# Expert weights in a mixture-of-experts stage: the order in which the queue is given the transfers

## The reference

```python
def expert_block(args):
    e, tok, g = args
    xb = ht[tok]
    hid = jax.nn.silu(xb @ w1[e]) * (xb @ w3[e])
    return (hid @ w2[e]) * g[:, None].astype(ht.dtype)
```

## Time and profile before

| | |
|---|---|
| median of 3 runs | 1514.43 us |
| profiled execution, its own time | 1511.4 us |
| its span, first to last instruction | 1509.6 us |
| TensorE busy | 1363.3 us (90%) |
| VectorE, ScalarE busy | 749.1 us (50%), 483.1 us (32%) |
| matmuls of L1577, of L1591 | 414.6 us, 201.0 us |
| weight DMAs (L742) | 192 of 1 MB, median 14.5 us from issue to landing |
| on the chain that ended last | L1577 8%, weight DMAs 5%, L1591 3% |

### The profile page before, as it was taken

How to read it: one execution, slowest core, us unless ns; L and a number is a source line. 1 busy time by engine, 2 the same in 40 slices (tenths; PEclk the granted TensorE clock), 3 DMA queues, 4 the chain that set the end, 5 groups by cost and what they waited for, 6 DMA issues and landing times. The chain is left out here.

```text
span 1509.6 us, 22993 instructions
## 1 busy us (share of the span) xinstructions
PE 1363.3 (90%) x6898; PEld 626.2 (41%) x6899; DVE 749.1 (50%) x1430; ACT 483.1 (32%) x771; POOL 126.7 (8%) x176
## 2 busy tenths in 40 slices
PE   4999998999988999999999499899899798998991
PEld 2555553445442333333333244488644232332330
DVE  2699999977773221222111453367647242233324
ACT  4101010134323442334232330266522153253421
POOL 0000000001220010011010300000002010010002
PEclk9999999899998999999999699999999899999996
DMA  9645581738059999698834500130094799999925
GB/s 348 203 161 176 187 306 42 287 119 292 29 203 362 384 398 397 242 331 327 298 125 153 204 1 0 41 73 2 2 364 144 287 347 395 397 382 395 398 103 181
DMA packets 163844, 342.73 MB, mean 227 GB/s; under 512 B 9120, under 2 KB 34320, under 8 KB 163792
## 3 DMA queue, kind: packets, MB, share of 16 engines
q1 hardware_dynamic: 146464, 298.03, 54.5%
q0 software_dynamic: 7440, 25.43, 4.6%
q10 hardware_dynamic: 9888, 18.62, 3.6%
HBM read 311.80 MB, written 30.24 MB: 227 GB/s over the span
## 5 line engine op out<-in xcount | busy, mean ns | idle before, releaser
L1577 PE MATMUL PS<-WR,XT 128*64 128x512 f32 x1760 | 414.6, 615 | 26.4 <-DVE WR L1713 16.9
L1577 PEld LDWEIGHTS PS<-WR,XT 128*64 128x64 f32 x1760 | 127.7, 141 | 263.1 <-issue 208.8
L1646 ACT ACTIVATE WR<-WR 128x2048 f32 x90 | 168.9, 1906 | 152.3 <-issue 142.8
L1725 DVE TENSOR_TENSOR HID<-PS,SIL 128x256 f32<-128x256 f32 x55 | 23.3, 424 | 364.1 <-ACT SIL L1657 364.1
L1591 PE MATMUL PS<-WR,HTT 128*64 128x512 f32 x880 | 201.0, 599 | 2.5 <-DVE HTT L1787 1.3
L1245 PE MATMUL PS<-HT,RING 128*128 128x512 f32 (+1 forms) x480 | 159.2, 494 | 0.7 <-DVEq L1368 0.5
L1713 DVE COPY WR<-WR 128x2048 f32 x90 | 108.2, 1228 | 98.4 <-DMA WR<-in_moe_w 40.3
L1392 DVE SCALAR_TENSOR_TENSOR AR<-AR,cols 128x783 f32 (+3 forms) x131 | 122.6, 936 | 0.0
L1245 PEld LDWEIGHTS PS<-HT,RING 128*128 128x128 f32 x480 | 91.0, 190 | 67.0 <-issue 61.1
L1392 DVE SCALAR_TENSOR_TENSOR ROWS<-AR,cols,ROWS 128x783 f32<-128x783 f32 (+2 forms) x123 | 115.1, 936 | 0.0
L1941 PE MATMUL PS<-RING,HT 128*128 128x512 f32 x224 | 99.5, 601 | 3.1 <-DVE HT L524 1.8
(11 more groups left out here) (249 smaller groups left out, 1388.8 us busy)
## 6 DMA issues: line engine op xcount, KB each, us to landing
WR<-in_moe_w SPq DMA_DIRECT2D x192, 1024.0 KB, 14.5
RING<-in_w_mod SPq DMA_DIRECT2D x24, 2048.0 KB, 15.0
moe_out<-YO ACTq DMA_DIRECT2D x110, 128.0 KB
RING<-in_conv_pw SPq DMA_DIRECT2D x16, 512.0 KB, 5.3
moe_out<-HT SPq DMA_DIRECT2D x16, 512.0 KB, 8.5
RING<-in_attn_w_qkv SPq DMA_DIRECT2D x3, 2048.0 KB, 12.8
ROWS<-rows_of_layer SPq DMA_DIRECT2D x11, 512.0 KB, 5.9
RING<-in_conv_pw SPq DMA_DIRECT2D x2, 2048.0 KB, 10.4
```

The source lines that it names most:

```text
L1577: ins = pe.matmul(PUV[g * SUB:(g + 1) * SUB, :], XT[:, k, :], W13[:, :, k, g * (FE // 2):(g + 1) * (FE // 2)], start=(k == 0), stop=(k == ...
L1646: return nc.scalar.activation(to, src, ACT.Copy)
L1725: nc.vector.tensor_tensor(HID[:, :], PUV[:, FE // 2:FE], SIL[:, :], ALU.mult).then_inc(hid_ready[L], 1)
```

## The change

The loop on SP runs over e from 2 to 16. It gives out the pair of expert e and then the down weights of expert e-1. The wait of each load is still for the copy that frees its home: `(e - 1) * 2` for the pair, and e-2 for the down weights of expert e-1. The number of transfers, their sizes and their homes are the same, and so are the instructions of every other engine. The loop's last round gives out only w2 of expert 15.

```diff
-                for e in range(1, NE):
-                    for kind, placed in ((1, (w1_placed,)), (3, (w3_placed,)),
-                                         (2, (w2_placed_low, w2_placed_high))):
-                        if kind != 2 and e <= L + 1:
-                            continue
-                        if e >= 3:
-                            for one in placed:
-                                sp.wait_ge(one[L], (e - 1) * (1 if kind == 2 else 2))
-                        load_weight(sp, L, e, kind)
+                for e in range(2, NE + 1):
+                    if L + 1 < e < NE:
+                        for kind, placed in ((1, w1_placed), (3, w3_placed)):
+                            if e >= 3:
+                                sp.wait_ge(placed[L], (e - 1) * 2)
+                            load_weight(sp, L, e, kind)
+                    if e >= 4:
+                        sp.wait_ge(w2_placed_low[L], e - 2)
+                        sp.wait_ge(w2_placed_high[L], e - 2)
+                    load_weight(sp, L, e - 1, 2)
```

## The result

The changed kernel took 1519.84 us, the median of 7 runs (1518.58 to 1521.36), against 1514.43 for 7 runs of the kernel before on the same chip (1509.93 to 1516.75): ratio 1.0046, 95% interval 1.0033 to 1.0058. The ratio is estimated from the single runs and is not the quotient of the two medians, which is 1.0036; in microseconds the medians differ by 5.4, and the interval stands for 5.0 to 8.8. The change is slower, and just outside my range. Its profiled execution took 1520.53 (span 1518.8). The file is one line longer: up is L1578 now (L1577 before), down L1592 (L1591), the hidden values' take L1663, the weight copies L1647 (ScalarE) and L1714 (VectorE).

The account below looks back on a forecast made before the run. Full DMA stretches in both layers bound the kernel, where queue place sets TensorE's waits. Layer 0 -1.2 us plus layer 1 0.0 made -1.2 on a median of 1514.4: 1513.2 us forecast, range 1507.5 to 1519.5.

Parts of the forecast that it names:

- the advance: How much earlier SP's whole weight queue runs in the new order: 5.4 us in layer 1, 6.7 us in layer 0.
- The advance, layer 1: Layer 1's queue runs 5.4 us earlier: 4.5 at w2 of expert 2 plus 0.9 at the pair behind the gap.
- The advance, layer 0: Layer 0's queue runs 6.7 us earlier: w2 of expert 2 ends at 492.0, old place filled at 497.8, plus 0.9.
- wait of 1.3 at expert 6: Layer 0, down of expert 6: w2 ready at 562.7, TensorE there at 561.4, so it waits 1.3 us.
- VectorE's chain: VectorE waits for w2's upper half with its product of hidden values behind it; the half comes about in time, no cost.
- The sum: Layer 0 -1.2 us plus layer 1 0.0 us gives -1.2 us on the profiled execution of 1511.4.
- The third: Rival: no queue advance, HBM bounds the total, place alone decides; +11.2 us, 1525.6; above +3 has chance 0.20, mostly 1518 to 1521.
- The first: Rival: down weights come in time, no down waits, only the pairs' gain shows; -9.6 us, 1504.8; chance 0.10.
- the second: Rival: same mechanism with a larger advance, each microsecond more giving one in each layer; 1508 to 1511; chance 0.20.
- the fourth: Rival: no effect, because the copies and not the queue set the waits; 1514.4; chance 0.50 together with the forecast.

Follow-up runs that it names:

- no_upper: The changed kernel with VectorE's copy of w2's upper half replaced by a short copy that waits for no transfer (result left wrong): 1515.59 us, 1 run.
- order_l0: The new order in layer 0's stage only, layer 1 as in the kernel before: 1517.73 us, ratio 1.0019 to the kernel before.
- again: The kernel before, unchanged in its old order, profiled once more: 1514.84 us, 1 run.
- by_blocks: Against the kernel before, w2 ahead of the next pair for experts of several blocks, behind it for single-block ones: 1512.96 us, ratio 1.0008.
- mixed: Against the kernel before, each w2 placed singly ahead of, within or behind the next pair, never two w2 side by side: 1502.44 us, ratio 0.9921.
- switch: New order for w2 of experts 1 to 3 (layer 1: 3 and 4), then the old order: 1518.43 us, ratio 1.0042 to the kernel before.

## Why the prediction was wrong
The mechanism was the forecast one: a place in a full queue, the gain before up, the new waits before down at the two-block experts. What failed is the size of one term, the advance, above all in layer 1, where it was 2.7 us and not 5.4; beside it one cost that I put at nothing (VectorE's chain, 1.7 us) and, in layer 0, 1.65 us of slow clock that a slightly smaller advance brought in.

**The advance, layer 1 (5.4 forecast, bounds 4.5 to 6.7).** Measured 2.7 at w2 of expert 12, outside the bounds. This is the step that failed most. It began short: w2 of expert 2, which I let follow the pair of expert 3 within 5.4 us, took 7.3, and at the pair of expert 4 the advance was 4.2, not 5.4. At expert 5 it was 4.0, and the new wait before its down 3.98 instead of about 2; 0.6 of that is the old place, which I had put at 1275.2 by even steps of 18.0 us and which was filled at 1275.8. Then the queue ran dry ahead of the pair of expert 10, where it fell from 5.3 to 2.6. I had asked where the old order lost queue time to late issues, and never where the new one would: with one w2 less ahead of it, a pair can reach the head of the queue while the copy that frees its home is still to come, as that of expert 10 did. Down of expert 12 then began at 1405.83 - 4.9 = 1400.9, 2.7 after the forecast 1398.2, which is the missing 2.7 of advance.

**The advance, layer 0 (6.7 forecast, bounds 4.5 to 7.5).** Measured 4.9, within the bounds. About 1.0 of the missing 1.8 was there at the pair of expert 3: w2 of expert 1, now third in the queue and put at nothing, was still ahead of it, and the pair took 15.7 us from issue to its last half (471.3 to 487.0), where I had taken 14.7 from layer 1. And the sum stood next to a step: 1.8 less of it turned a wait of 1.6, which I had called too short to cost clock, into one of 3.32, and 16 matmuls took 5.30 us. My lower bound, an advance of 4.5 for +1.0, left that step out: with an advance of 4.9 the first down is ready at 531.4 - 4.9 + 2.4 = 528.9, 0.7 ahead of the old 529.62, and the 1.65 of slow clock makes it +0.9. Forecast -1.2; measured +0.9 between the two profiles, which agrees, but the old order's own three profiles of layer 0 spread over 2.3 us. The forecast wait of 1.3 at expert 6 did not come: its copy began at 561.0 (forecast 560.3), and TensorE was late enough by then.

**VectorE's chain (forecast nothing: "comes about in time").** It cost 0.31 and 1.42 us behind experts 12 and 14; no_upper, without the wait for that half, had neither. I had followed the upper half only as far as down, and not the w3 copy queued behind it.

**The sum.** Layer 1: 2.6 at the end of the first down of expert 12 (0.0 forecast), 0.3 and 1.4 for VectorE's chain; with 1.0 by which the stage's first block was longer (its 32 up matmuls took 9.36 us against 8.35) that is the 5.3 of the table. That 1.0 stands ahead of everything that the change moves. The old order shows both lengths (9.44 us in order_l0, 8.18 in again), so I count it as no part of the effect. Between the stages the two profiles differ by 3.3 us, with the same instructions: TensorE was idle for 40.6 us before and 40.4 after, and the same matmuls took 310.5 and 314.0 us at a granted clock of 0.94 and 0.93. So by these rows the 3.3 is matmul time at a lower clock. I count it as no part of the effect either, but that is not shown: with the old order in layer 0 this stretch took 351.2 to 353.0 us in three profiles, with the new one 352.7 to 354.4 in four. What is left, +0.9 and +4.3, is 5.2, where the medians differ by 5.4 and the ratio gives 5.0 to 8.8. Against the mean of the old order's three profiles it would be +0.5 and +4.0. The agreement with the medians is closer than single profiles can warrant.

**The rivals.** The third held: its condition was that both advances be about 2 us short, and they were short by 1.8 and 2.7; its time for that, 1518 to 1521, holds the result. Its stated reason, no advance at all, did not hold. I had given it 0.20. The first (no down waits) and the second (a larger advance) fell with the rows above, the fourth with the waits that went and the 5.4 us. That a later transfer might pass an earlier one did not show either: in each profiled run the 192 weight halves landed in the order of issue. The Trainium skill (DMA: Bandwidth & Descriptors, Queues, rings and completion order) allows such passing; no run here shows it for 1 MB halves of one queue.

**What stays open.** Why w2 of expert 2 took 7.3 us was not tried. The queue was not empty: from 1219.2 to 1226.4 us the DMA engines moved 2.89 MB at 402 GB/s, of which the w2 is 2.10 and another queue's transfers 0.26. Whether the new order in layer 0 costs more than its own stage shows (order_l0: 2.9 us by the ratio, 1.6 in the stage against the old order's mean) is open too. That the dry queue at expert 10 alone made the 2.7 us there is read from the trace; no run took it away alone.

## What to carry to other kernels
When transfers in one full queue change places, work out for each one both when it lands and when its buffer lets it be issued: a queue gains only if the new order has something to move at every point where a copy frees a home. A gain that lies next to a step in the cost (here a wait of about 2 to 3 us, which can bring slow clock) is worth its sign on either side, so sum both cases. And one rule for all items was wrong in both directions here: placing each down weight by when it is needed, without two of a kind side by side, gave 0.8% where neither of the other fixed orders (w2 behind the pair, w2 within it) gained anything.

## What the runs showed of the hardware
I had taken a wait of about 2 us as enough for slow clock. Its length alone does not decide. In by_blocks this wait of 1.96 us was followed by a granted clock of 0.65, that is partly at 1.2 GHz, and the wait of 3.24 by full clock, 2.4 GHz:

```profile
526.79 5.35 PE L1586 MATMUL PS<-WR,XT 128*64 128x512 f32 x16 [1.96 <-DVE WR L1722]
...
1270.11 3.65 PE L1586 MATMUL PS<-WR,XT 128*64 128x512 f32 x16 [3.24 <-DVE WR L1722]
```

```profile
1270.50:1273.50 3.00, 3.00 (x16) 0.86 (x12) 1.31 (x2) 0.00 (x0) 0.00 (x0) 1.00 1.04 406
527.00:530.00 3.00, 3.00 (x10) 0.78 (x8) 0.98 (x1) 0.00 (x0) 0.00 (x0) 0.65 1.04 385
```

In mixed, waits of 2.05 and 2.17 cost no clock and one of 5.64 did. A wait of 2.08 us came both ways: in the kernel before the 16 matmuls behind it took 5.35 us, in switch 3.65 (at 531.38). So the prediction's price, 1.5 to 1.7 us for a wait between 2 and 4 us, is one that is paid at times for waits of about 2 to 3 us, and not a sure one.
